# A three-part kernel on one Trainium2 core: squares of tiles 12 and 13 joined on VectorE, and three side flows moved by one or two steps

## The reference

```python
def layer_norm(x, g, b):
    mu = jnp.mean(xf, axis=-1, keepdims=True)
    var = jnp.mean(jnp.square(xf - mu), axis=-1, keepdims=True)
    y = (xf - mu) * lax.rsqrt(var + LN_EPS)
def rmsnorm(x, g):
    return xf * lax.rsqrt(jnp.mean(xf * xf, axis=-1, keepdims=True) + EPS) * g
```

## Time and profile before

| | |
|---|---|
| median of three runs | 3018.09 us (3013.39 to 3019.24) |
| the profiled execution | 3018.98 us |
| its span | 3017.7 us |
| granted TensorE clock, mean | 0.998 of full speed |
| busy: TensorE, VectorE, ScalarE, GpSimd | 2973.1, 2154.8, 1431.2, 654.4 us |
| read from memory | 623.48 MB |

### The profile page before, as it was taken

How to read it: one execution, slowest core, us unless ns; L and a number is a source line. 1 busy time by engine, 2 the same in 40 slices (tenths; PEclk the granted TensorE clock), 3 DMA queues, 4 the chain that set the end, 5 groups by cost and what they waited for, 6 DMA issues and landing times. The chain is left out here.

```text
span 3017.7 us, 57841 instructions
## 1 busy us (share of the span) xinstructions
PE 2973.1 (99%) x25815; PEld 2548.6 (84%) x25840; DVE 2154.8 (71%) x2107; ACT 1431.2 (47%) x1399; POOL 654.4 (22%) x749
## 2 busy tenths in 40 slices
PE   9999999999999999999999999999999999999998
PEld 8888888888888888668888888888768688876887
DVE  6767877777766577656778777754776465898684
ACT  5433555554433464554645555543654454322553
POOL 0555255555445400000030000000040000012310
PEclk9999999999999999999999999999999999999999
DMA  8898588888898756545676666756454555666333
GB/s 301 295 318 307 196 293 312 298 306 296 296 329 290 267 187 202 185 161 174 205 254 240 213 234 223 245 198 207 143 169 161 176 178 199 230 240 220 134 128 138
DMA packets 306137, 690.15 MB, mean 229 GB/s; under 512 B 16576, under 2 KB 20800, under 8 KB 300128
## 3 DMA queue, kind: packets, MB, share of 16 engines
q1 hardware_dynamic: 270976, 564.20, 54.5%
q0 software_dynamic: 34912, 122.25, 11.4%
HBM read 623.48 MB, written 61.87 MB: 227 GB/s over the span
## 5 line engine op out<-in xcount | busy, mean ns | idle before, releaser
L688 PE MATMUL PSG<-XH,WS 128*128 128x256 bf16 x11264 | 1822.5, 273 | 8.6 <-DVE WS L2038 5.8
L1783 DVE TENSOR_TENSOR WS<-WF,WS 128x2048 bf16<-128x2048 f32 x485 | 1194.3, 2483 | 536.5 <-ACT WS L1183 535.9
L688 PE MATMUL PSG<-XL,WS 128*128 128x256 bf16 x5632 | 1472.5, 273 | 0.0
L688 PEld LDWEIGHTS PSG<-XH,WS 128*128 128x128 bf16 x11264 | 1101.6, 98 | 148.4 <-issue 14.9
L1183 ACT ACTIVATE WS<-WF 128x2048 bf16<-128x2048 f32 x485 | 910.5, 1899 | 584.9 <-PE PSG L688 209.5
L688 PE MATMUL PSG<-SCR,WS 128*128 128x256 bf16 x6720 | 737.9, 273 | 0.0
L688 PEld LDWEIGHTS PSG<-SCR,WS 128*128 128x128 bf16 x6720 | 656.7, 98 | 78.3
L688 PEld LDWEIGHTS PSG<-XL,WS 128*128 128x128 bf16 x5632 | 551.0, 98 | 66.0 <-DVE XL L1914 0.2
L595 POOL TENSOR_TENSOR SCR<-SCR 128x1024 bf16<-128x1024 f32 x88 | 228.1, 2592 | 8.0 <-DMA weight_halves<-SCR 6.6
L688 PE MATMUL PSG<-WS,XH 128*128 128x512 bf16 x620 | 181.2, 380 | 4.2 <-ACT XH L1319 2.2
L2093 DVE SCALAR_TENSOR_TENSOR SCR<-PSG,PR,SCR 128x254 f32<-128x254 f32 (+1 forms) x352 | 142.4, 472 | 15.5 <-ACT SCR L1427 14.9
(11 more groups left out here) (283 smaller groups left out, 1650.7 us busy)
## 6 DMA issues: line engine op xcount, KB each, us to landing
WF<-ffn_w_up SPq DMA_DIRECT2D x176, 1024.0 KB, 6.7
WF<-ffn_w_down SPq DMA_DIRECT2D x88, 1024.0 KB, 6.5
WF<-ab_w_in SPq DMA_DIRECT2D x56, 1024.0 KB, 5.1
WF<-a_w_in SPq DMA_DIRECT2D x44, 1024.0 KB, 7.2
weight_halves<-SCR POOLq DMA_DIRECT2D x176, 256.0 KB, 6.0
WS<-weight_halves SPq DMA_DIRECT2D x44, 1024.0 KB, 4.8
SCR<-cd_w_in POOLq DMA_DIRECT2D x80, 512.0 KB, 7.0
WF<-a_w_out SPq DMA_DIRECT2D x16, 1024.0 KB, 7.3
```

What stands on the lines that cost most here:

```text
L688: return nc.tensor.matmul(o, lhsT, rhs, start=start, stop=stop, skip_group_check=True)
L1783: tt(l, w, h, ALU.subtract).then_inc(s_lo, 1)
```

## The change

It has four parts. (1) In all five norms VectorE adds the squares of tiles 12 and 13 to SUMS[1] (`add_two_squared`), TensorE sums SUMS[1] once, behind the last output tile, and the two single-tile sums are gone; `hold` is set in the third norm too. (2) `rms_first` idles two steps instead of three in front of each scaled piece, on ScalarE and VectorE. (3) TensorE's S5 flow idles five steps instead of four behind its first product. (4) On all three engines two empty steps are put in front of the queue before the last gate group. Each norm now counts four on s_sqrd instead of three, so later counts are renumbered.

```diff
 # TensorE, layer_residual
                     if m == 2:
                         side.drain()
-                        sum_squares(3 * L + 3, False)
                     if m == 3:
                         sum_values(2 * L + 2, 2, False)
-                        nc.tensor.wait_ge(s_sq, 5 * L + 4)
-                        sum_tiles(1, SQ[1][:, 0:2, :], False, False)
+                        sum_squares(4 * L + 4, False)
...
 # TensorE, s5
                 product(0)
-                yield from idle(4)
+                yield from idle(5)
...
 # TensorE, ScalarE and VectorE, before the last gate group
             gemm(stage["cd_gate"][2], xh, xl, rate=4)
+            side.add_first(idle(2))
             gemm(stage["cd_gate"][3], xh, xl, rate=4)
...
 # TensorE, final_tail
                 if m == 2:
                     side.drain()
-                    sum_squares(23, False)
                 if m == 3:
-                    nc.tensor.wait_ge(s_sq, 32)
-                    sum_tiles(1, XN2[1][:, 0:2, :], False, False)
+                    sum_squares(28, False)
...
 # ScalarE and VectorE, rms_first
                 for p in range(4):
-                    yield from idle(3)
+                    yield from idle(2)
                     scaled_high(0, p, 4 * p, gi, XN0)
...
 # VectorE
+            def add_two_squared(n, sq):
+
+                t = own.mark(tt(sq[:, 0, :], sq[:, 0, :], sq[:, 1, :], ALU.add))
+                nc.vector.wait_ge(s_sqrd, n)
+                nc.vector.wait_ge(v_own, t)
+                tt(SUMS[:, 1, :], SUMS[:, 1, :], sq[:, 0, :], ALU.add).then_inc(s_sqrd, 1)
...
 # VectorE, layer_residual
-                    ps = gemm(gi, rate=rate, before=None if g else before, hold=L == 0 and g == 3)
+                    ps = gemm(gi, rate=rate, before=None if g else before, hold=L in (0, 2) and g == 3)
...
                         tt(SUMS[:, 0, :], SUMS[:, 0, :], STAT[:, 2, :], ALU.add).then_inc(s_sums, 1)
+                        nc.vector.wait_ge(s_sq, 5 * L + 4)
+                        add_two_squared(4 * L + 3, SQ[1])
                         nc.vector.wait_ge(s_mm, done(gi))
                         tt(x[:, 2:4, :], x[:, 2:4, :], ps[:, 2:4, :], ALU.add).then_inc(evacuated(gi), 1)
...
 # VectorE, the last group
                     tt(x[:, 0:2, :], ps[:, 0:2, :], x[:, 0:2, :], ALU.add).then_inc(s_cen, 1)
+                    nc.vector.wait_ge(s_sq, 32)
+                    add_two_squared(27, XN2[1])
                     nc.vector.wait_ge(s_mm, done(gi))
```

More of the change, by code:

```diff
@@ L836, in rms_squares @@
                 yield from idle(6)
-                sum_squares(20, True)
+                sum_squares(24, True)
                 yield
@@ L950, in rms_sums @@
                 yield from idle(19)
-                sum_squares(16, True)
+                sum_squares(20, True)
                 yield
@@ L1226, in layer_stats @@
                     nc.scalar.wait_ge(*evac(gi))
-                    nc.scalar.wait_ge(s_sqrd, 3 * L + 1)
+                    nc.scalar.wait_ge(s_sqrd, 4 * L + 1)
                     act(SQ[0], tiles(2), ACT.Square).then_inc(s_sq, 1)
@@ L1238, in layer_residual @@
                 side.drain()
-                nc.scalar.wait_ge(s_sqrd, 3 * L + 2)
+                nc.scalar.wait_ge(s_sqrd, 4 * L + 2)
                 nc.scalar.wait_ge(s_cen, 3 * L + 3)
@@ L1247, in rms_stats @@
                 if g >= 2:
-                    nc.scalar.wait_ge(s_sqrd, 16 + g - 1)
+                    nc.scalar.wait_ge(s_sqrd, 20 + g - 1)
                 if r == 0 and g == 3:
@@ L1325, in rms_first @@
                     if g >= 2:
-                        nc.scalar.wait_ge(s_sqrd, 12 + g - 1)
+                        nc.scalar.wait_ge(s_sqrd, 16 + g - 1)
                     act(SQF[g % 2], tiles(g), ACT.Square).then_inc(s_sq, 1)
@@ L1741, in final_stats @@
                 if g == 2:
-                    nc.scalar.wait_ge(s_sqrd, 21)
+                    nc.scalar.wait_ge(s_sqrd, 25)
                 act(XN2[g % 2], tiles(g), ACT.Square).then_inc(s_sq, 1)
@@ L1755, in scalar_program @@
             side.drain()
-            nc.scalar.wait_ge(s_sqrd, 22)
+            nc.scalar.wait_ge(s_sqrd, 26)
             nc.scalar.wait_ge(s_cen, 13)
@@ L1832, in add_squares @@
                     nc.vector.wait_ge(s_sq, 5 * L + q + 1)
-                    add_squared(3 * L + q, SQ[q % 2], None if q else 3 * L)
+                    add_squared(4 * L + q, SQ[q % 2], None if q else 3 * L)
                 nc.vector.wait_ge(*evac(gi))
@@ L1895, in rms_stats @@
                     nc.vector.wait_ge(s_sq, 24 + g + 1)
-                    add_squared(16 + g, SQ[g % 2], None if g else 13)
+                    add_squared(20 + g, SQ[g % 2], None if g else 13)
                     if g == 2:
@@ L1999, in rms_first @@
                     nc.vector.wait_ge(s_sq, 20 + g + 1)
-                    add_squared(12 + g, SQF[g % 2], None if g else 12)
+                    add_squared(16 + g, SQF[g % 2], None if g else 12)
                     if g < 2:
@@ L2442, in vector_program @@
             nc.vector.wait_ge(s_sq, 28)
-            add_squared(19, SQG[1])
+            add_squared(23, SQG[1])
             def s5():
@@ L2606, in final_stats @@
                 nc.vector.wait_ge(s_sq, 28 + g + 1)
-                add_squared(20 + g, XN2[g % 2], None if g else 14)
+                add_squared(24 + g, XN2[g % 2], None if g else 14)
                 yield
```

## The result

The changed kernel took 2998.06 us (median of four runs, 2996.70 to 3000.03), the kernel before in the same comparison 3016.34 (3013.39 to 3019.24, four runs): a ratio of 0.9941, 95% interval 0.993 to 0.9953. The prediction was 3007.0 with a range from 3001.0 to 3014.5. The profiled executions are 2998.78 (span 2997.5) and 3018.98 (span 3017.7), 20.2 apart.

The account below looks back on a forecast made before the run. The prediction took TensorE, busy 99% of the span, as the bound. Its terms, 3.1 - 2.2 + 1.0 + 9.7 = 11.6 us off 3018.98, gave 3007.4, stated as 3007, with a range from 3001 to 3014.5.

Parts of the forecast that it names:

- Step 2: Value projection vb: old waits of 3.36 us go, new waits of 5.6 for weight halves come; 2.2 lost.
- Step 4: Eight heads of the last recurrence: scores move apart, so most of 11.0 us of waits go; 9.7 gained.
- Step 1: Five norms: fewer matmuls of squares on TensorE, VectorE's added adds mostly hidden; 3.1 us gained.
- The sign named for the third norm: Third norm: its centring would start right behind a weight half.
- The further 1.4 at the sixth chunk: vb: the weight half after the fifth chunk's ends at 2205.5 against a demand at 2204.1, 1.4 us more wait.
- Step 3: State-space part: three waits of 1.8 us together go, a new one of about 0.8 comes; 1.0 gained.
- The 0.5 for the last head: Last of the eight heads: a weight half in front of VectorE's weighing makes it late; 0.5 us lost.
- rival A: Eight heads: slower VectorE weighing makes TensorE wait 1.0 in six heads; total gain 5.6, 3013.4 us; chance 0.16.
- From the last gate group on: Last heads: two further empty steps keep first and second scores 2.62 us or more apart.
- B: vb does not lose, the fifth chunk's half is in time; gain 13.8 to 16, 3003 to 3005; chance 0.15.
- C: Shifted steps meet the same waits elsewhere; only norms gain, less vb: 0.9, 3018 us; chance 0.09.
- D: Slower: the late half at vb drains the three raw weight buffers; 32 us lost, 3037; chance 0.04.

Follow-up runs that it names:

- no_hold: The changed kernel with `hold` for the first norm alone, so the third norm's weight half is in its old place; 2998.67 us, ratio 0.9946.
- squares: The kernel before with part 1 alone (squares of the norms joined, `hold` in the third norm); 3011.29 us, ratio 0.9988.
- idle5: The kernel before with part 3 alone (TensorE's S5 flow idles five steps instead of four); 3001.70 us, ratio 0.9955.
- shifts: The kernel before with parts 3 and 4 together; 3003.10 us, ratio 0.9963.
- gate_only: The kernel before with part 4 alone (two empty steps before the last gate group); 3014.89 us, ratio 0.9999.
- no_pieces: The changed kernel with three empty steps again in front of each scaled piece; 3001.96 us, ratio 0.9951.
- late_decay: The kernel late_decay2 with four empty steps instead of two between the last scaled piece and the decay; 2998.89 us, ratio 0.9946.
- late_decay2: The changed kernel with two empty steps between the last scaled piece and the decay, on ScalarE and VectorE; 2995.36 us, ratio 0.9933.
- apart: late_decay2 with ScalarE's decay activations behind one more weight copy and VectorE's next decay part one step later; 2994.25 us, ratio 0.993.
- no_shifts: The changed kernel without part 4 (no two empty steps before the last gate group); 2998.16 us, ratio 0.9943.
- after_again: The changed kernel itself, run and profiled once more; 2998.30 us, ratio 0.9942.
- pieces: The kernel before with part 2 alone (two empty steps instead of three before each scaled piece); 3015.21 us, ratio 1.0003.

## Why the prediction was right or wrong

The mechanisms that the steps named were right. Four things in the sum were wrong or missing, and together they put the time outside the range. The sum started from 3018.98, 4.2 above the median of many runs. Step 2 put a loss of 2.2 where 0.1 was gained: it stopped at vb's end and left out the first head of the recurrence, which gives 3.3 back. Step 4 priced a wait at its idle time, 0.97, and it is worth 1.18. The output's 0.8 had no term.

**Step 1, norms: right.** 2.9 against 3.1, each norm within 0.1 of its term. The adds on VectorE were hidden where step 1 said, and no_hold shows what happens where they are not. The sign named for the third norm is there too: its centring starts at 1420.24, right when the held half ends. What step 1 did not have is the 0.8 behind the last norm.

**Step 2, vb: the mechanism right, its neighbour left out.** The step forecast a wait of 4.2 at the fifth chunk because the decay's activations stand in front of a weight copy; it was 4.28. The further 1.4 at the sixth chunk was hidden, since the fifth ran 2.7 longer at the lower clock, which no term had. Together vb lost 3.3, more than the 2.2 forecast. But the step stopped at vb's end. Behind it the waits of 1.16 and 1.69 of the recurrence's first head, with 0.2 behind each, are worth 3.3, and they went. The net is 0.1 gained.

Why they went the traces show, though no run was made for it. The weighing of that head, VectorE's work that TensorE waits for, does not come earlier: it starts at 2224.26 before and at 2223.59 after, with TensorE 0.96 ahead. It is shorter, 6.44 before and 3.72 after. GpSimd's decays start with the end of the scan, and the weighing starts 18.1 behind that end before and 24.8 after (scan's end 2206.20 and 2198.82). The last rows of the decays, before and after:

```profile
2229.91 0.44 POOL L566 TENSOR_TENSOR SCR<-SCR 128x128 f32<-128x128 f32 x1
```

```profile
2223.89 0.44 POOL L566 TENSOR_TENSOR SCR<-SCR 128x128 f32<-128x128 f32 x1
```

```profile
2223.59 3.72 DVE L2292 TENSOR_TENSOR SCR<-SCR 128x128 f32<-128x128 f32 x16
```

Before, the whole weighing ran beside them; with the scan further ahead of it only its first 0.8 us does. All fourteen traces stand in this order:

| trace | of the weighing beside GpSimd, us | weighing | TensorE's two waits |
|---|---|---|---|
| before, squares, idle5, shifts, gate_only, no_pieces | all | 6.44 to 6.45 | 1.16 and 1.69 |
| late_decay | 6.2 | 6.26 | 1.05 and 1.49 |
| late_decay2 | 5.8 | 6.07 | 0.81 and 1.28 |
| apart | 4.9 | 5.66 | 0.61 and 0.88 |
| no_hold, no_shifts | 2.6, 2.1 | 4.53, 4.34 | none |
| after_again, after | 1.2, 0.8 | 3.92, 3.72 | none |
| pieces | 0 | 3.33 | none |

So the step that failed had followed what the moved work holds up, and not what waited for it on GpSimd.

**Step 3, state-space part: right.** 1.1 against 1.0, and the new wait for L2505 is 0.9 where 0.8 was said.

**Step 4, heads: mechanism right, each wait undersized.** All waits named went, and the period of a head is 15.40. The step priced each at the idle time of its row, 0.97. These are the rows of the kernel before:

```profile
2813.20 0.60 PE L688 MATMUL PB<-SCR,ONE 128*128 128x256 f32 x2
2814.77 2.02 PE L688 MATMUL PB<-SCR 128*128 128x128 f32 x16 [0.97 <-DVE SCR L2295]
```

By starts, which the text ahead of the prediction calls the measure of a matmul, the wait costs 2814.77 - 2813.20 = 1.57 where the changed kernel has 2804.20 - 2803.74 = 0.46: 1.11. The row's 0.60 holds 0.14 of way through the array that the next matmul would have overlapped. The 16 matmuls behind the wait take 2.02 instead of 1.95, another 0.07. That is 1.18, and 15.40 for the period instead of 15.61. Ten waits with 0.21 more each give 11.0 + 2.1 = 13.1; the waits that are left, 0.60 and 0.37 with the same addition, take off 1.4: 11.7, and 11.9 was measured. In both, 0.8 is the first head's 0.59 with its restart, which was to stay and was by chance gone in the first profile; without it the sum is 10.9, the measured gain 11.1 and the forecast 9.7. The 0.5 for the last head was right (0.60).

The exponential again started 0.02 behind its table load, and no wait for ScalarE appeared in the heads. The drain that the Trainium skill (ScalarE: Activation LUTs, What ACT_TABLE_LOAD costs) adds to each load is not seen at this place, as the row had said. Nor did rival A's slower weighing come: the second head's took 4.56 before and 4.56 after, beside GpSimd's decays, and the longest in the eight heads after the change is 4.70. The exclusive lock of the Trainium skill (SBUF — State Buffer, Who interferes with whom) had spoken for a longer one. The rows of the recurrence's first head show both engines going on beside each other: 16 products on VectorE took 3.33 with GpSimd still and 6.45 with its products beside all of them.

Part 4 was given a share, "From the last gate group on". It has none: idle5 alone reaches what idle5 with it does, and by itself it trades the waits for one of 3.19.

**The base of the sum: wrong by 4.** The sum was taken from the profiled execution of 3018.98, near the median of three runs, 3018.09. Over 24 runs the median is 3014.73, 4.2 lower. The trace of before holds three things that come and go: waits for weight halves of 2.7 (3.3 by starts against idle5), against 1.0 in the changed kernel's first profile and none in idle5, squares or after_again; 1.7 of low clock behind a wait of 2.2 that is in all fourteen traces and was followed by the low clock in three (before, idle5, late_decay); and the 0.8 of the heads. They add up to 5.8; an execution near the median holds some of it too, and how much was not measured. The first two could be read in the trace of before, and neither was. With the base at 3014.7 and the forecast's own 11.6 the predicted time would have been 3003.1; with all stages at their measured size, 16.0, it is 2998.7.

Of the rivals, B (vb does not lose) came true by its result and not by its reason: the half was late, and the recurrence's first head paid. A, C and D did not occur. B's time of 3003 to 3005, with the right base, would have been 2999 to 3001.

## What to carry to other kernels

A wait's price is the distance between two starts with it less the distance without it; the idle time in the bracket leaves out the overlap that was lost, and behind it a little restart, here 0.2 on every wait of 1. When a step is moved earlier, write down who waits for its result as well as who stands behind it in the queue, or the gain of the move is missing from the sum; and look at what will then run beside what, on VectorE and GpSimd above all. And before a sum is made against a profiled execution, look in it for waits on loads and for low-clock stretches that the change doesn't touch: with only three runs beside it, they are what sets the base.

A helper's work that must wait for another engine belongs behind the weight copies that can run meanwhile, on both engines separately. That turned a step worth about nothing (part 2) into one worth 4.1 us by the medians and 5.1 by the traces.

## What the runs showed of the hardware

In windows of 4 us over all fourteen traces, the granted clock fell below 0.97 ahead of the last 35 us of a run only at waits of TensorE of 2.06 us and more (the waits of 5.4 to 6.0 at the very start lie ahead of the clock's record). At the waits of 4.3 to 4.7 us (pieces at 500 us and at vb; at vb the changed kernel twice, no_shifts, no_hold) it always did, to a lowest window of 0.50 to 0.75 (1.00 is 2.4 GHz, 0.50 is 1.2 GHz), and that cost 2.7 in the one worked out. At 3.19 it did (gate_only, 0.66). At 2.1 to 2.2 it did in some executions: three of fourteen at L2379, and at vb in late_decay but not in late_decay2; at the 2.19 in the heads (before, pieces, squares) it never did, nor at waits of 1.7 and less. So a wait near 2 us has a price that differs from run to run. That removing one also narrows the scatter is not shown; apart's five runs lie within 1.5 us, late_decay2's within 4.0.

The same 16 products of 128x128 on VectorE took from 3.33 to 6.45 us, by how much of them GpSimd's products of the same shape ran beside (table in step 2).
